# The experts' gather: plain float32 tokens, or their two rounded parts

## The chip, the cores and the metric

The kernel runs on one core of one Trainium2 chip. The metric is the device time of one execution in microseconds (us); the kernel before has a median of 2643.16 us over three runs. TensorE (PE in the profile) multiplies, VectorE (DVE) and ScalarE (ACT) work element by element, GpSimd (POOL) does little here, and SyncE (SP) issues the transfers from HBM.

## The reference

The program is two small models in a row, on 256 tokens of width 1024. The change lies in the last layer of the first, a mixture of eight experts. Cut to that:

```
def moe_ffn(h, router, w_gu, w_down):
    logits = (h @ router).astype(jnp.float32)
    top_val, top_idx = lax.top_k(logits, TOP_K)
    weights = jax.nn.softmax(top_val, axis=-1)
    gate = jnp.sum(jax.nn.one_hot(top_idx, N_EXPERTS, dtype=jnp.float32) * weights[..., None], axis=-2)
    out = jnp.zeros(h.shape, jnp.float32)
    for e in range(N_EXPERTS):
        out = out + gate[..., e:e + 1] * swiglu(h, w_gu[e], w_down[e])
    return out
```

`h` is the normed input, modulated: `rmsnorm(x, norm_w) * (1 + scale) + shift`. Two of eight experts (TOP_K) take each token; an expert is 1024 to 2 x 3584 and 3584 to 1024. All inputs and outputs are float32.

## The kernel before

The kernel is a row of stages; `experts` (L2362) is the fifth. Each engine runs its own function per stage (`tensor`, `vector`, `scalar`, `sync`), in program order, and semaphores tie them together: `e.wait_ge(*M.v.at(("Pe", x)))` waits until VectorE has passed the event of that name.

Products are made exact enough by splitting. A weight unit of 128x2048 float32 is copied by ScalarE to the rounded type fp32r (`split_hi`, L351; the high part) and VectorE subtracts that from the original (`split_lo`, L363; the low part). TensorE multiplies high x high, high x low and low x high in fp32r. Weights come from HBM through three slots of 2 MB; a slot comes free when VectorE has made the low part of its last unit, and a part's buffer comes free when TensorE has used it (three buffers of each).

Each expert works on at most 128 of the 256 tokens. Which ones is decided once: TensorE multiplies the tokens with the router (`routed_tensor`, L2665), VectorE ranks the logits into `sel` and takes the positions of the chosen tokens into `pos` (`routed_vector`, L2691). From `sel` and `pos` VectorE makes, for each expert, `Pe`, a [128, 2, 128] matrix of zeros and ones (L2384, `gather_vector`): row t has a one in column s where token t is the expert's s-th. TensorE then

- transposes Pe (`gather_tensor`, step 1), for putting the results back later, and
- gathers (steps 2 and 3, L2446): for each of 8 column tiles k and each half hf of the tokens, `xn[:, hf, k]` is the stationary operand and `Pe[:, hf, :]` the moving one, both plain float32; the two halves add up in PSUM. One step is a block of four k, 8 products.

VectorE scales and shifts the gathered columns into `XGf` (step 3 and 4) and the two parts `XGh`, `XGl` are made from it (step 5), which the expert's weight products use.

Order: for the first expert all of these steps come one after another, ahead of any weight product. For the others `coming` (L2627) puts step l-29 behind the down-projection's unit l of the expert before, so that a block of gather products stands in TensorE's queue between weight products. An expert has 42 units (28 of the up-projection, 14 of the down-projection), 12 weight products of 512 columns each. `round_tensor`, `round_scalar` and `round_vector` (L2632 to L2663) write this order out. A second round over the experts runs only if one expert has more than 128 tokens, and it isn't run on these inputs.

Ahead of the rounds, `scalar` (L2789) and `vector` (L2805) norm the tokens into `xn`, and modulate the transposed tokens into `HT` for the router (`turned_half`, L2758, one half of the pieces each); ScalarE and VectorE split weight unit 0 still earlier, and unit 1 right after `turned_half`.

Of the kernel before, what the change touches and what calls it, by code (L numbers as in the profile page):

```python
# [6 lines left out]
F32 = mybir.dt.float32  # L7
R32 = mybir.dt.float32r
AF = mybir.ActivationFunctionType
AX = mybir.AxisListType  # L10

D = 1024
# [502 lines left out]
def norm_scalar(c, e, S, ready):  # L515

    e.wait_ge(*c.first.g.at("eps"))
    e.table()
    for h in range(2):
        e.wait_ge(*ready[h])  # L520
        e.activation(c.xn[:, h, :], c.X[:, h, :], AF.Square, accum_out=c.ssq[:, h:h + 1]).then_inc(*S.a.up())
        e.wait_ge(*S.a.now())
        e.activation(c.rst[:, h:h + 1], c.ssq[:, h:h + 1], AF.Ln, scale=1.0 / D, bias=c.eps[:, :]).then_inc(*S.a.up())
        e.wait_ge(*S.a.now())
        e.activation(c.rst[:, h:h + 1], c.rst[:, h:h + 1], AF.Exp, scale=-0.5).then_inc(*S.a.up(("rst", h)))
# [1836 lines left out]
def experts(c):  # L2362
# [3 lines left out]
    io, K, X, xn, ones, gates = c.io, c.K, c.X, c.xn, c.ones, c.gates  # L2366
    before = c.mamba
    M = c.moe = Stage(c, "moe")
# [12 lines left out]
    hTh, hTl = c.put(40.5, "ehTh", [128, 28, 128], R32), c.put(54.5, "ehTl", [128, 28, 128], R32)  # L2381
    XGh, XGl = c.put(106.5, "XGh", [128, KC, 128], R32), c.put(110.5, "XGl", [128, KC, 128], R32)
    XGf, Y = HT[:, 0:4, :].rearrange("p a (b s) -> p (a b) s", s=128), HT[:, 4:8, :].rearrange("p a b -> p (a b)")
    Pe = c.put(68.5, "Pe", [128, 2, 128])  # L2384
    hrow = [c.put(70.5 + 2 * i, f"hrow{i}", [128, 512]) for i in range(2)]
    router_landed, norm_landed, raw_landed = c.event_signal("router_landed", 16), c.event_signal("final_norm_landed", 16), c.event_signal("raw_landed", 16)
    fn = gates[1]
# [43 lines left out]
    def gather_tensor(e, S, blk, x, step):  # L2431
        if step == 1:
            ps = ubanks.take((S.name, "PT", x))
            e.wait_ge(*ps.was)
            e.wait_ge(*S.v.at(("Pe", x)))
            for hf in range(2):
                m = e.transpose(ps.t[:, hf * 128:(hf + 1) * 128], Pe[:, hf, :], K["ident"])
            m.then_inc(*S.t.up(("PT", x)))
        if step in (2, 3):
            k0 = 4 * (step - 2)  # L2440
            ps = ubanks.take((S.name, "XG", x, k0))
            e.wait_ge(*ps.was)
            e.wait_ge(*S.v.at(("Pe", x)))
            for k in range(k0, k0 + 4):
                for hf in range(2):
                    m = e.matmul(ps.t[:, (k - k0) * 128:(k - k0 + 1) * 128], xn[:, hf, k * 128:(k + 1) * 128], Pe[:, hf, :], hf == 0, hf == 1)  # L2446
            m.then_inc(*S.t.up(("XG", x, k0)))

    def gather_vector(e, S, blk, x, step):
# [29 lines left out]
    def gather_scalar(e, S, blk, x, step):  # L2479
        if step == 5:  # L2480
            if x:
                e.wait_ge(*S.t.at(("row", x - 1, 6, 1)))
            for k0 in (0, 4):
                e.wait_ge(*S.v.at(("XGf", x, k0)))
                e.activation(XGh[:, k0:k0 + 4, :], XGf[:, k0:k0 + 4, :], AF.Copy).then_inc(*S.a.up(("XGh", x, k0)))
# [94 lines left out]
    def use_scalar(e, S, n):  # L2580
        x, l = at(n)
        if l < 28:
            j = l // 4
            if l % 4 == 1 and j:
                hidden_scalar(e, S, x, j - 1)
            if l % 4 == 3:
                ps = c.psum.of((S.name, "row", x, j, 0))
                e.wait_ge(*S.t.at(("row", x, j, 0)))
                if j > 1:
                    e.wait_ge(*S.t.at(("hT", x, j - 2)))  # L2590
                elif x:
                    e.wait_ge(*S.t.at(("hT", x - 1, 6 - j % 2)))
                e.activation(hrow[j % 2][:, :], ps.t[:, :], AF.Silu).then_inc(*S.a.up(("silu", x, j)))
                c.psum.leave((S.name, "row", x, j, 0), S.a)
        elif l == 28:
            hidden_scalar(e, S, x, 6)

    def use_vector(e, S, n):
        x, l = at(n)
        if l < 28:  # L2600
            j = l // 4
            if l % 4 == 1 and j:
                hidden_vector(e, S, x, j - 1)
            if l % 4 == 3:
                ps = c.psum.of((S.name, "row", x, j, 1))
                e.wait_ge(*S.t.at(("row", x, j, 1)))
                e.wait_ge(*S.a.at(("silu", x, j)))
                e.tensor_tensor(hrow[j % 2][:, :], hrow[j % 2][:, :], ps.t[:, :], ALU.mult).then_inc(*S.v.up(("h", x, j)))
                c.psum.leave((S.name, "row", x, j, 1), S.v)
            if l == 3 and x:  # L2610
                put_vector(e, S, x - 1)
            return
        if l == 28:
            hidden_vector(e, S, x, 6)
        if l == PER - 1 and (x < NE - 1 or S is again):
            summed_vector(e, S, x)
# [10 lines left out]
    def coming(n):  # L2627

        x, l = at(n)
        return (x + 1, l - 29) if 29 <= l < 35 and x + 1 < NE else None  # L2630
# [10 lines left out]
    def round_scalar(e, S, W, blk, begun):  # L2641
        for n in range(NU + AHEAD):
            if (EARLY if S is M else 0) <= n < NU:
                W.split_hi(e, n)
            if n == AHEAD - 1:
                begun(e)
            if n >= AHEAD:
                use_scalar(e, S, n - AHEAD)
                if coming(n - AHEAD):
                    gather_scalar(e, S, blk, *coming(n - AHEAD))  # L2650

    def round_vector(e, S, W, blk, begun):
        for n in range(NU + AHEAD):
            if (EARLY if S is M else 0) <= n < NU:
                W.split_lo(e, n)
            if n == AHEAD - 1:
                begun(e)
            if n >= AHEAD:
                use_vector(e, S, n - AHEAD)
                if coming(n - AHEAD):  # L2660
                    gather_vector(e, S, blk, *coming(n - AHEAD))
# [76 lines left out]
    def second(e, signals, otherwise=None):  # L2738

        e.wait_ge(*M.v.at("flag"))  # L2740
        return e.only_if(fli[0:1, 0:1], [s.at("end") for s in signals], otherwise)
# [16 lines left out]
    def turned_half(e, S, sig, dve):  # L2758

        e.wait_ge(*c.side.v.at(("mod", "moe", "cols")))  # L2760
        for n in ((0, 2) if dve else (1, 3)):
            h, k0 = n // 2, n % 2 * 4
            hs = slice(h * 128, (h + 1) * 128)
            ps = c.psum.of((S.name, "turned", n))
            e.wait_ge(*S.t.at(("turned", n)))
            for k in range(4):
                o, i = HT[:, k0 + k, hs], ps.t[:, k * 128:(k + 1) * 128]
                if dve:
                    e.tensor_scalar(o, i, s1[:, k0 + k:k0 + k + 1], ALU.mult, s2[:, k0 + k:k0 + k + 1], ALU.add).then_inc(*sig.up(("HT", n)))
                else:  # L2770
                    e.activation(o, i, AF.Identity, scale=s1[:, k0 + k:k0 + k + 1], bias=s2[:, k0 + k:k0 + k + 1]).then_inc(*sig.up(("HT", n)))
            c.psum.leave((S.name, "turned", n), sig)
# [16 lines left out]
    def scalar(e):  # L2789
        e.wait_ge(*before.t.at(("y", 7)))  # L2790
        for n in range(EARLY):
            U.split_hi(e, n)
        norm_scalar(c, e, M, [before.v.at(("X", h)) for h in range(2)])
        before.wait_for(e, "end")
        turned_half(e, M, M.a, False)
        round_scalar(e, M, U, 0, routed_scalar)
        M.a.mark("end")
        with second(e, [again.a]):
            M.wait_for(e, "end")
            round_scalar(e, again, U2, 1, lambda e: [gather_scalar(e, again, 1, 0, s) for s in range(6)])  # L2800
        again.a.mark("end")
        e.wait_ge(*again.v.at("end"))
        norm_scalar(c, e, again, [M.v.at(("X_half", h)) for h in range(2)])

    def vector(e):  # L2805
        norm_vector(c, e, M, 1)
        before.wait_for(e, "end")
        turned_half(e, M, M.v, True)
        round_vector(e, M, U, 0, routed_vector)
        begun = M.v.n  # L2810

        def last_put():
            M.v.n = begun
            summed_vector(e, M, NE - 1)
            put_vector(e, M, NE - 1)
            M.v.mark("end")

        with second(e, [again.v], last_put):
            last_put()
            M.wait_for(e, "end")  # L2820
            round_vector(e, again, U2, 1, lambda e: [gather_vector(e, again, 1, 0, s) for s in range(6)])
            put_vector(e, again, NE - 1)
        again.v.mark("end")
        e.wait_ge(*norm_landed.at("norm"))
        for h in range(2):
            e.wait_ge(*again.a.at(("rst", h)))
            e.scalar_tensor_tensor(X[:, h, :], X[:, h, :], c.rst[:, h:h + 1], fn[:, :], ALU.mult, ALU.mult).then_inc(*again.v.up(("X", h)))
# [990 lines left out]
```

## Time and profile before

| | |
|---|---|
| median of 3 runs | 2643.16 us (2642.90 to 2644.75) |
| the profiled execution | 2645.73 us, its span 2643.9 us |
| TensorE busy | 2432.2 us, 92% of the span |
| VectorE busy | 1984.5 us, 75% |
| ScalarE busy | 1431.7 us, 54% |
| read from HBM | 605 MB, 229 GB/s over the span |
| the experts' stage | about 776 to 1812 us |

The profile is of one execution. Busy time is the sum of an engine's instructions; a matmul's end is modelled and matmuls are pipelined, so that the start of one to the start of the next tells what it costs, not its duration. LDWEIGHTS (PEld) is the load of the stationary operand, 128x128 here, which TensorE can do while an earlier matmul streams. The granted clock is a share of 2.4 GHz.

### The profile page before, as it was taken

How to read it: one execution, taken by the hardware profiler on the slowest of the kernel's cores; microseconds unless marked ns; L12 is line 12 of the kernel's file. 1: busy time of each engine (PE TensorE's matmuls, PEld its weight loads, DVE VectorE, ACT ScalarE, POOL GpSimd, SP SyncE). 2: the span in 40 equal slices, each digit the busy share in tenths (PEclk: the TensorE clock that was granted, in tenths of full speed). 3: DMA queues.
4: the chain of work that ended last, by engine and by line, in shares of the span. 5: the costliest groups of instructions: out<-in, count | busy, mean ns of one | idle time of the engine just before them, and what ended most of it. 6: DMA issues, size and time to landing. Idle time of an engine off the chain costs nothing.

```text
span 2643.9 us, 32969 instructions
## 1 busy us (share of the span) xinstructions
PE 2432.2 (92%) x13898; PEld 2108.3 (80%) x13898; DVE 1984.5 (75%) x2208; ACT 1431.7 (54%) x1594; POOL 209.3 (8%) x261
## 2 busy tenths in 40 slices
PE   4877899898889999999999999998897999897998
PEld 3756799787777888888888888887887997886997
DVE  6756777686657898888888989886666775767675
ACT  3312443464546776767676767674444653344562
POOL 1101001000000000000000000001311110221110
PEclk8886899897889999999999999999998999998999
DMA  9652678432256999999999999995224453323552
GB/s 318 216 196 88 215 271 302 158 139 81 96 182 232 348 360 347 358 348 360 352 356 337 369 338 367 342 365 191 69 96 159 164 190 134 108 76 118 195 184 77
DMA packets 263558, 608.44 MB, mean 230 GB/s; under 512 B 18472, under 2 KB 33082, under 8 KB 263402
## 3 DMA queue, kind: packets, MB, share of 16 engines
q1 hardware_dynamic: 247808, 554.39, 58.4%
q0 software_dynamic: 14640, 51.49, 5.8%
q8 instruction: 111, 1.82, 0.3%
q10 hardware_dynamic: 954, 0.37, 0.1%
q14 instruction: 45, 0.37, 0.0%
HBM read 605.17 MB, written 1.05 MB: 229 GB/s over the span
## 4 chain that ended last, share of the span: by engine, by line
PE 80%; DVE 10%; ACT 5%; DMA 2%; issue 1%; POOL 1%; SPq 0%; PEldq 0%; PEld 0%; DVEq 0%; ACTq 0%; POOLq 0%
PE ps L132 78%; PE ps L136 2%; DVE eb L153 1%; DMA slots<-in_hyb_mod_w 1%; DVE X L153 1%; ACT L142 1%; DMA beside<-in_dense_mod_w 1%; DVE ul_in L145 1%; DVE macc L153 1%; DVE xn L153 1%; ACT uh_ffn L139 0%; ACT eb L139 0%; ACT xn L139 0%; DVE ul_ssm_w L145 0%; DVE gate L153 0%
## 5 line engine op out<-in xcount | busy, mean ns | idle before, releaser
L145 DVE TENSOR_TENSOR ul_moe_w<-slots,uh_moe_w 128x2048 fp32r<-128x2048 f32 x334 | 762.6, 2290 | 108.7 <-ACT uh_moe_w L139 108.4
L139 ACT ACTIVATE uh_moe_w<-slots 128x2048 fp32r<-128x2048 f32 x334 | 640.2, 1917 | 215.8 <-PE ps L132 187.4
L132 PE MATMUL ps<-uh_moe_w,XGh 128*128 128x512 f32 x896 | 356.7, 398 | 3.1 <-DVE XGl L145 2.1
L132 PE MATMUL ps<-uh_moe_w,XGl 128*128 128x512 f32 x896 | 349.5, 390 | 0.0
L132 PE MATMUL ps<-ul_moe_w,XGh 128*128 128x512 f32 x896 | 349.0, 389 | 0.0
L145 DVE TENSOR_TENSOR ul_ffn<-slots,uh_ffn 128x2048 fp32r<-128x2048 f32 x62 | 142.1, 2292 | 101.1 <-ACT uh_ffn L139 101.1
L132 PE MATMUL ps<-HTf,uh_ffn 128*128 128x256 f32 x704 | 201.5, 286 | 2.8 <-DVE HTlf L145 2.8
L132 PE MATMUL ps<-HTlf,uh_ffn 128*128 128x256 f32 x704 | 201.0, 285 | 0.0
L132 PE MATMUL ps<-HTf,ul_ffn 128*128 128x256 f32 x704 | 200.9, 285 | 0.0
L132 PEld LDWEIGHTS ps<-uh_moe_w,XGh 128*128 128x128 f32 x896 | 168.3, 188 | 39.1 <-DVE XGl L145 2.2
L132 PEld LDWEIGHTS ps<-uh_moe_w,XGl 128*128 128x128 f32 x896 | 168.2, 188 | 35.8
L132 PEld LDWEIGHTS ps<-ul_moe_w,XGh 128*128 128x128 f32 x896 | 168.5, 188 | 35.1 <-issue 1.7
L139 ACT ACTIVATE uh_ffn<-slots 128x2048 fp32r<-128x2048 f32 x66 | 125.7, 1911 | 96.4 <-PE ps L132 96.4
L132 PE MATMUL ps<-uh_moe_w,ehTh 128*128 128x512 f32 x448 | 177.2, 396 | 0.0
L132 PE MATMUL ps<-ul_moe_w,ehTh 128*128 128x512 f32 x448 | 174.7, 390 | 0.0
L132 PEld LDWEIGHTS ps<-HTf,uh_ffn 128*128 128x128 f32 x704 | 137.1, 195 | 3.6 <-DVE HTlf L145 3.6
L132 PE MATMUL ps<-uh_moe_w,ehTl 128*128 128x512 f32 x448 | 138.1, 389 | 0.0
L132 PEld LDWEIGHTS ps<-HTlf,uh_ffn 128*128 128x128 f32 x704 | 137.2, 195 | 0.0
L132 PEld LDWEIGHTS ps<-HTf,ul_ffn 128*128 128x128 f32 x704 | 137.0, 195 | 0.0
L132 PE MATMUL ps<-HTm,uh_in 128*128 128x256 f32 (+1 forms) x352 | 106.0, 301 | 6.1 <-DVE ul_in L145 3.0
L145 DVE TENSOR_TENSOR ul_dense_w<-slots,uh_dense_w 128x2048 fp32r<-128x2048 f32 x33 | 75.5, 2291 | 45.0 <-ACT uh_dense_w L139 45.0
L145 DVE TENSOR_TENSOR ul_ssm_w<-slots,uh_ssm_w 128x1024 fp32r<-128x1024 f32 (+1 forms) x57 | 68.6, 1204 | 54.0 <-ACT uh_ssm_w L139 53.9
(509 smaller groups left out, 5576.4 us busy)
## 6 DMA issues: line engine op xcount, KB each, us to landing
slots<-in_moe_w_gu SPq DMA_DIRECT2D x111, 2048.0 KB, 8.8
slots<-in_moe_w_down SPq DMA_DIRECT2D x56, 2048.0 KB, 7.9
slots<-in_w_up SPq DMA_DIRECT2D x20, 2048.0 KB, 7.9
slots<-in_w_in SPq DMA_DIRECT2D x14, 2048.0 KB, 8.5
slots<-in_dense_w_gu SPq DMA_DIRECT2D x10, 2048.0 KB, 9.9
slots<-in_ssm_w_in SPq DMA_DIRECT2D x10, 2048.0 KB, 8.0
slots<-in_w_down SPq DMA_DIRECT2D x10, 2048.0 KB, 7.8
slots<-in_dense_w_down SPq DMA_DIRECT2D x5, 2048.0 KB, 12.7
```

The costliest lines, as they stand in the source:

```text
L132: return self.e.matmul(o, lhsT, rhs, start=start, stop=stop, skip_group_check=skip) if self.e else DONE
L136: return self.e.transpose(o, i, ident[0:n, 0:n]) if self.e else DONE
L139: return self.e.activation(o, i, f, **kw) if self.e else DONE
L142: return self.e.preload_act_table_set("natural_log_exp_and_others") if self.e else DONE
L145: return self.e.tensor_tensor(o, a, b, op) if self.e else DONE
L153: return self.e.scalar_tensor_tensor(o, a, s, b, op0, op1) if self.e else DONE
```

## The change

The tokens `xn` are split once, as the weights are: ScalarE copies each half into `xh` (fp32r), and VectorE subtracts that from `xn` into `xl` (fp32r). Both get places of 8 KB per partition. In the gather each product with `xn` becomes two, one with `xh` and one with `xl`, and the four of a column tile add up in PSUM. `Pe` is declared fp32r, and its transpose reads it as float32. ScalarE's two copies stand between `turned_half` and its round, VectorE's two subtractions too, behind a wait for TensorE's last transposes of `xn` and for the copies. TensorE waits for the subtractions ahead of each block (after the first time, the wait is left out).

```
-    Pe = c.put(68.5, "Pe", [128, 2, 128])
+    Pe = c.put(68.5, "Pe", [128, 2, 128], R32)
+    xh, xl = c.put(118.25, "xnh", [128, 2, D], R32), c.put(126.25, "xnl", [128, 2, D], R32)
...
-                m = e.transpose(ps.t[:, hf * 128:(hf + 1) * 128], Pe[:, hf, :], K["ident"])
+                m = e.transpose(ps.t[:, hf * 128:(hf + 1) * 128], Pe[:, hf, :].bitcast(F32), K["ident"])
...
             e.wait_ge(*ps.was)
+            e.wait_ge(*M.v.at("xl"))
             e.wait_ge(*S.v.at(("Pe", x)))
             for k in range(k0, k0 + 4):
+                o, cs = ps.t[:, (k - k0) * 128:(k - k0 + 1) * 128], slice(k * 128, (k + 1) * 128)
                 for hf in range(2):
-                    m = e.matmul(ps.t[:, (k - k0) * 128:(k - k0 + 1) * 128], xn[:, hf, k * 128:(k + 1) * 128], Pe[:, hf, :], hf == 0, hf == 1)
+                    e.matmul(o, xh[:, hf, cs], Pe[:, hf, :], hf == 0, False)
+                    m = e.matmul(o, xl[:, hf, cs], Pe[:, hf, :], False, hf == 1)
...
         turned_half(e, M, M.a, False)
+        for h in range(2):
+            e.wait_ge(*M.v.at(("xn", h)))
+            e.activation(xh[:, h, :], xn[:, h, :], AF.Copy).then_inc(*M.a.up(("xh", h)))
         round_scalar(e, M, U, 0, routed_scalar)
...
         turned_half(e, M, M.v, True)
+        e.wait_ge(*M.t.at(("turned", 3)))
+        for h in range(2):
+            e.wait_ge(*M.a.at(("xh", h)))
+            e.tensor_tensor(xl[:, h, :], xn[:, h, :], xh[:, h, :].bitcast(F32), ALU.subtract).then_inc(*M.v.up("xl"))
         round_vector(e, M, U, 0, routed_vector)
```

## Rows read from the trace of the kernel before

**Rows 1.** The page: busy time and share by engine; the chain by line.
```profile
PE 2432.2 (92%) x13898; PEld 2108.3 (80%) x13898; DVE 1984.5 (75%) x2208; ACT 1431.7 (54%) x1594; POOL 209.3 (8%) x261
...
PE ps L132 78%; PE ps L136 2%; DVE eb L153 1%; DMA slots<-in_hyb_mod_w 1%; DVE X L153 1%; ACT L142 1%; DMA beside<-in_dense_mod_w 1%; DVE ul_in L145 1%; DVE macc L153 1%; DVE xn L153 1%; ACT uh_ffn L139 0%; ACT eb L139 0%; ACT xn L139 0%; DVE ul_ssm_w L145 0%; DVE gate L153 0%
```

**Rows 2.** Busy time by stretch of the experts' stage (one of six like stretches).
```profile
core 0: us, PE busy (x) PEld busy (x) DVE busy (x) ACT busy (x) POOL busy (x), PEclk, DMA share, GB/s
...
930.00:1054.00 124.00, 124.00 (x570) 101.42 (x569) 110.22 (x76) 86.78 (x58) 0.00 (x0) 1.00 0.96 352
```

**Rows 3.** Waits from 780 to 1800 us: us in total, times, longest.
```profile
ACT uh_moe_w L139 <- PE ps L132: 187.4, 240, 3.9
...
PE ps L132 <- DVE XGl L145: 2.1, 1, 2.1
```

**Rows 4.** Timeline of the stage's start: start, us, engine, line, instructions [idle before].
```profile
781.04 2.72 DVE L150 TENSOR_SCALAR HT<-ps,s_moe 128x128 f32<-128x128 f32 x8
...
784.64 1.92 ACT L139 ACTIVATE uh_moe_w<-slots 128x2048 fp32r<-128x2048 f32 x1
...
784.86 6.96 PE L132 MATMUL ps<-rw,HT 128*128 128x8 f32 x32 [1.64 <-issue]
786.59 2.29 DVE L145 TENSOR_TENSOR ul_moe_w<-slots,uh_moe_w 128x2048 fp32r<-128x2048 f32 x1 [2.82 <-ACT uh_moe_w L139]
788.91 0.37 SPq L177 DMA_DIRECT2D slots<-in_moe_w_gu  x1
791.86 0.17 DVE L156 COPY L<-ps 128x16 f32<-128x16 f32 x1 [2.98 <-PE ps L132]
...
796.43 0.60 DVE L150 TENSOR_SCALAR Pe<-k_iota,epos,esel 128x128 f32<-128x128 f32 x2
...
797.57 5.63 PE L132 MATMUL ps<-Pe,xn 128*128 128x128 f32 x32
...
805.26 0.50 PE L132 MATMUL ps<-uh_moe_w,XGh 128*128 128x512 f32 x1 [2.06 <-DVE XGl L145]
...
805.83 0.40 PE L132 MATMUL ps<-uh_moe_w,XGl 128*128 128x512 f32 x1
...
806.06 0.40 PE L132 MATMUL ps<-uh_moe_w,XGh 128*128 128x512 f32 x1
```

**Rows 5.** The gather's products: ns min/median/max; one steady block in time.
```profile
L132 PEld LDWEIGHTS ps<-Pe,xn x256: 187/192/337, 797.4 to 1654.2; 128*128 128x128 f32 x128
L132 PE MATMUL ps<-Pe,xn x256: 270/275/421, 797.6 to 1654.3; 128*128 128x128 f32 x128
...
897.50 1.95 PE L132 MATMUL ps<-Pe,xn 128*128 128x128 f32 x16
899.20 0.48 PE L132 MATMUL ps<-uh_moe_w,ehTh 128*128 128x512 f32 x1
```

**Rows 6.** The page's group of weight loads with XGl: busy us, mean ns.
```profile
L132 PEld LDWEIGHTS ps<-uh_moe_w,XGl 128*128 128x128 f32 x896 | 168.2, 188 | 35.8
```

**Rows 7.** The second model's attention in time: plain products that stream 64 columns.
```profile
1967.50 1.90 PE L132 MATMUL ps<-vbt,PTm 128*128 128x64 f32 x16
1969.20 0.47 PE L132 MATMUL ps<-uh_in,HTm 128*128 128x512 f32 x1
```

**Rows 8.** Router products, then first gather, by stretch (columns end as rows 2).
```profile
784.86:791.80 6.94, 6.94 (x32) 6.86 (x32) 0.00 (x0) 0.50 0.25 62
...
797.36:803.20 5.84, 5.84 (x34) 5.65 (x33) 0.00 (x0) 0.64 0.00 0
```

**Rows 9.** A stretch of 48 rounded products of 256 columns: TensorE, clock, DMA.
```profile
1819.34:1825.10 5.76, 5.76 (x50) 1.00 0.12 44
```

**Rows 10.** A copy to fp32r and a subtraction of 128x1024: ns min/median/max.
```profile
L139 ACT ACTIVATE uh_in<-slots x58: 256/1046/1062, 1809.0 to 2387.0; 128x1024 fp32r<-128x1024 f32 x56, 128x64 fp32r<-128x64 f32 x2
L145 DVE TENSOR_TENSOR ul_in<-slots,uh_in x58: 225/1218/1592, 1809.3 to 2388.1; 128x1024 fp32r<-128x1024 f32 x56, 128x64 fp32r<-128x64 f32 x2
```

**Rows 11.** A stretch around the first gather, columns as rows 2.
```profile
797.00:805.30 8.30, 6.15 (x35) 5.96 (x35) 3.79 (x11) 1.29 (x3) 0.00 (x0) 0.73 0.00 0
```

## The prediction

> **What bounds the kernel now.** I read the page first. TensorE is busy 92% of the span, and the chain that ended last lies for 78% of it on the one line that issues every matmul [rows 1]. The change touches the experts' stage, so the busy time by stretches is next: in each of six like stretches from 930 to 1674 us TensorE is busy for all of the 124 us, at a granted clock of 1.00 (2.4 GHz), while the DMA engines are busy 96 to 97% of the time, VectorE about 110 us and ScalarE about 87 us [rows 2]. The waits of the stage say the same from the other side: ScalarE waits 187.4 us for TensorE to release a weight buffer, while the longest wait of TensorE's weight products is one of 2.1 us, at the very start [rows 3]. So in steady state what ends last is TensorE, with the transfers close behind; time on TensorE counts in full there, time on VectorE or ScalarE counts only when it eats up the lead that they have. The start of the stage is different. There the chain hops: VectorE modulates, TensorE computes the router's logits (6.94 us), VectorE ranks, TensorE counts positions, VectorE builds Pe, TensorE gathers, and TensorE's first weight product starts only at 805.26 [rows 4]. On that stretch every engine's latency is on the path, unless it lies beside the logits.
>
> **The change part by part.**
>
> *1. The product itself, on TensorE.* The loop runs 8 experts x 2 blocks of four column tiles; a block has 4 x 2 products of a 128x128 tile of tokens with a 128x128 tile of Pe. That is 128 plain products, and the trace has 256 weight loads and 256 matmuls for them [rows 5]: a plain float32 product is two load-and-stream records. The change replaces each by two products of the rounded type, and those have one record each (the experts' weight products with XGl: 8 experts x 28 units x 4, and 896 records [rows 6]). So a block has 16 records before and 16 records after. The question is what one record costs with 128 columns.
> Before, a block in steady state takes from 897.50 to 899.20, 1.70 us, or 106 ns a record [rows 5]. Two things could set that: streaming (two passes over 128 columns) or loading 128x128 weights. The trace separates them: in the second model's attention, plain products stream only 64 columns against 128x128 weights, half the streaming, and 16 records again take from 1967.50 to 1969.20, 1.70 us [rows 7]. The router's products stream 8 columns and take 6.94/32 = 217 ns a record at the granted clock 0.50 (1.2 GHz), which is 108 ns at 2.4 GHz [rows 4, 8]. So 106 ns is the floor that a 128-column weight load sets, whatever is streamed behind it. A load for rounded operands lasts 188 ns on average, one for plain float32 has a median of 192 ns [rows 5, 6]; nothing there says that a rounded load is shorter.
> No row shows a rounded product over 128 columns; all have 256 or 512. That price is bounded from both sides. Upper end: 48 rounded products of 256 columns take from 1819.34 to 1825.10, 120 ns each [rows 9], and fewer columns should not cost more. Lower end: 512 columns cost 227 ns (805.83 to 806.06 [rows 4]), 256 cost 120 ns, so 107 ns per 256 columns; taking off another 128 gives 67 ns, if the load did not count. I take 106 ns, from the 64-column rows, because there too the stream is shorter than the load, as it would be here. Then each block stays at 1.70 us and the part is worth 0. With the upper end a block costs 16 x 0.014 = 0.22 us more; seven experts in steady state have 14 blocks, 3.1 us, and the first expert's two blocks (32 records in 5.63 us [rows 4], at a clock of 0.64 over the stretch [rows 8]) grow by 0.13 of that, 0.7 us: +3.8 us. With the lower end a record saves 0.039 us: 14 x 16 x 0.039 = 8.7 us, and 0.37 x 5.63 = 2.1 us at the start: -10.8 us.
> One rule speaks against this value. The Trainium skill, "TensorE: Matmul & The Clock Gate", section "Back-to-back issue gap", puts load-and-matmul pairs at about 81 ns for 128 columns and 131 ns for 512; by that the sum would be an estimate of 14 x 16 x 0.025 + 1.3 = 6.9 us less. For 512 columns this trace has 227 ns, not 131, so I do not carry its 81 over.
>
> *2. The two parts, made once.* ScalarE gets two copies of 128x1024 to the rounded type and VectorE two subtractions of that size; the same two forms for the second model's input weights take 1046 and 1218 ns (medians) [rows 10]. ScalarE's copies stand right ahead of its split of weight unit 1, which starts at 784.64 now [rows 4]. Both copies: 784.7 to 786.8; unit 1's high part then ends near 788.8 instead of 786.56. VectorE ends its transposed tokens at 783.76, subtracts from 785.8 to 788.25, and makes unit 1's low part from 788.8 to 791.1 instead of 786.59 to 788.88. Next on VectorE is the copy of the logits, at 791.86, which waits for TensorE [rows 4]. The whole part hides beside the 6.94 us of logits with 0.8 us to spare; ScalarE's next work is an exponential that needs those logits. If that cover were gone, the added time on VectorE would be up to 2 x 1.22 us, on the path. VectorE's new wait for the last transposes has ended before its own last modulated tile, and TensorE's new wait for the two subtractions (done at 788.25, its gather begins at 797.57) ends long before. What is queued behind VectorE's wait for the copies is only unit 1's low part, already counted.
> Its consequence on the transfer queue: the refill of slot 0, issued at 788.91 when unit 1's low part was done [rows 4], goes out some 2.2 us later. Nothing is queued up behind it: the DMA engines are idle from 797 to 805.3, all through the gather (share 0.00 [rows 11]). Landing 2.2 us later, it only fills a part of that. Zero; two microseconds if it mattered.
>
> *3. Pe as a rounded tile.* Zeros and ones are the same numbers. Writing it is the same tensor_scalar on VectorE, 0.60 us for two [rows 4]. If writing the rounded type were twice as slow, it would be 0.6 us on the first expert's path, and nothing later, where a Pe is built while TensorE has weight products queued; at the other end it is 0. As many elements are written as before and the transposes read the same bits, so I take 0.1 us, near the lower end.
>
> **The sum.** 0 (product) + 0 (parts) + 0 (refill) + 0.1 (Pe) = +0.1 us on the profiled execution's 2645.73 us (span 2643.9 and 1.8 around it). The median of the runs shown is 2643.16; the forecast against it is 2643.3.
>
> **The rivals.**
> *A, slower: a rounded product over 128 columns costs what the plain one costs.* TensorE may take its single-pass rate for the rounded type only for long streams; every rounded product in this kernel streams 256 or 512 columns [rows 6, 9], so the trace can't exclude it. Its place is the gather, its price is the plain product's, two records or 213 ns, instead of one: a block doubles from 1.70 to 3.40 us, 14 x 1.70 = 23.8 us, and the first pair adds 5.6 us: +29.4 us, 2672.6. It decides as soon as a rounded 128-column product takes over 130 ns (14 x 16 x 0.024 us = 5.3 us). For it: no row excludes it. Against it: a rounded 256-column product takes 120 ns, little more than one pass of 256 columns, so no pass is hidden in the type itself.
> *B, faster: the rounded load overlaps.* If rounded weights load behind the preceding stream more fully, a record falls towards 67 ns and the total by up to 10.8 us, to 2632.4. The transfers would not stop it: at 96 to 97% busy they leave some 3% of a stretch of 124 us, 3.7 us, and B wants 1.3 us of that. (By the 81 ns of the Trainium skill, "TensorE: Matmul & The Clock Gate", section "Back-to-back issue gap", the time would be an estimate of 2636; no run here shows it.) For B: in weight products a load of 188 ns lies wholly behind a 227 ns stream. Against: with short streams no row of 128 weight columns falls below 106 ns.
> *C, the split at the start is not covered.* The margin is 0.8 us; a late copy on ScalarE would push the logits' copy by up to 2 us. This stays within the forecast's own range.
>
> **How the numbers follow.** The forecast (no change, C included) gets 0.70, A 0.18, B 0.12. The forecast's own range is 2640 (records a little cheaper) to 2649 (+3.8 for 120 ns records and +2 for C). Adding B takes the low end to 2632, and then 0.18 is left out, so the range is 2632 to 2649; A's 2673 lies outside it. A measurement of this kernel can tell about 0.2%, 5.3 us: the forecast's case is inside that but for its edges. So: faster 0.13 (B), same 0.68, slower 0.19 (A, and the edge at 120 ns with C).
>
> **What would show it.** In the trace after, Pe's group should have 256 records again, half with xnh and half with xnl, plus the 16 of the transposes. A steady block should take 1.7 us between the weight products around it; 1.07 would be B, 3.4 A. The logits' copy on VectorE should still wait for TensorE, with unit 1's low part ending near 791, and the first weight product should start 20.4 us after the first router product, within 0.3 us (784.86 and 805.26 [rows 4]). The last expert's last gather load, now at 1654.2 [rows 5], should again come 848.9 us after the first weight product. The prediction is wrong if the record isn't bound by its load, or if the stage is bound by its transfers after all, in which case even A or B would be partly hidden.

## The result and the profile after

The changed kernel has a median of 2651.99 us over 22 runs, the kernel before 2642.78 us over 22 on the same chip: a ratio of 1.0031, interval 1.0017 to 1.0045. In this measurement it is slower, the interval lying above 1.000, and the time is outside the range of 2632 to 2649. The same kernel was measured twice more (below): 1.0007 (0.9993 to 1.0021) and 1.0017 (0.9997 to 1.0037). Neither of these two can be told from no change by itself, and either ratio times 2643 us would lie inside the range. The three intervals overlap from 1.0017 to 1.0021, 4.5 to 5.5 us. What all three profiles of the changed kernel show is 3.7 to 3.8 us, in the stage's start, and the low clock that goes with it ends within 30 us of the router's first product.

The gather's products first, as in [rows 5]: their group, then one steady block and the weight product behind it, all in the changed kernel.

```profile
L132 PEld LDWEIGHTS ps<-Pe,xnh x128: 187/192/337, 799.5 to 1660.2; 128*128 128x128 f32 x128
L132 PE MATMUL ps<-Pe,xnh x128: 220/274/455, 799.6 to 1660.3; 128*128 128x128 f32 x128
...
L132 PEld LDWEIGHTS ps<-Pe,xnl x128: 187/192/333, 799.7 to 1660.3; 128*128 128x128 f32 x128
L132 PE MATMUL ps<-Pe,xnl x128: 274/276/415, 799.8 to 1660.4; 128*128 128x128 f32 x128
...
903.37 0.22 PE L132 MATMUL ps<-Pe,xnh 128*128 128x128 f32 x1
903.43 0.28 PE L132 MATMUL ps<-Pe,xnl 128*128 128x128 f32 x1
903.54 0.27 PE L132 MATMUL ps<-Pe,xnh 128*128 128x128 f32 x1
...
904.99 0.28 PE L132 MATMUL ps<-Pe,xnl 128*128 128x128 f32 x1
905.10 0.45 PE L132 MATMUL ps<-uh_moe_w,ehTh 128*128 128x512 f32 x1
905.39 0.40 PE L132 MATMUL ps<-ul_moe_w,ehTh 128*128 128x512 f32 x1
```

There are 256 records again. A block takes from 903.37 to 905.10, 1.73 us; before it was 1.70 us. A rounded product of 128 columns costs 111 ns (903.43 to 904.99 are 14 of them); a plain record in the gathers of the kernel before starts 108 to 112 ns after the one before it, with a median of 112. The steady state is as it was: VectorE makes Pe for the second and the eighth expert 750.85 us apart; in the kernel before the same two start at 893.80 and 1644.43, 750.63 us apart.

```profile
899.67 0.60 DVE L150 TENSOR_SCALAR Pe<-k_iota,epos,esel 128x128 fp32r<-128x128 f32 x2
...
1650.52 0.60 DVE L150 TENSOR_SCALAR Pe<-k_iota,epos,esel 128x128 fp32r<-128x128 f32 x2
```

Now the start of the stage, the timeline that answers [rows 4].

```profile
786.80 2.01 ACT L139 ACTIVATE xnh<-xn 128x1024 fp32r<-128x1024 f32 x2
...
787.02 6.96 PE L132 MATMUL ps<-rw,HT 128*128 128x8 f32 x32 [1.64 <-issue]
787.97 2.36 DVE L145 TENSOR_TENSOR xnl<-xn,xnh 128x1024 fp32r<-128x1024 f32 x2 [2.04 <-ACT xnh L139]
...
790.64 2.29 DVE L145 TENSOR_TENSOR ul_moe_w<-slots,uh_moe_w 128x2048 fp32r<-128x2048 f32 x1 [0.31 <-ACT uh_moe_w L139]
792.96 0.37 SPq L177 DMA_DIRECT2D slots<-in_moe_w_gu  x1
794.02 0.17 DVE L156 COPY L<-ps 128x16 f32<-128x16 f32 x1 [1.09 <-PE ps L132]
...
798.60 0.60 DVE L150 TENSOR_SCALAR Pe<-k_iota,epos,esel 128x128 fp32r<-128x128 f32 x2
...
799.60 0.46 PE L132 MATMUL ps<-Pe,xnh 128*128 128x128 f32 x1
799.85 0.41 PE L132 MATMUL ps<-Pe,xnl 128*128 128x128 f32 x1
...
808.72 0.80 PE L132 MATMUL ps<-uh_moe_w,XGh 128*128 128x512 f32 x1 [2.06 <-DVE XGl L145]
809.32 0.63 PE L132 MATMUL ps<-ul_moe_w,XGh 128*128 128x512 f32 x1
809.74 0.63 PE L132 MATMUL ps<-uh_moe_w,XGl 128*128 128x512 f32 x1
...
814.00 0.39 PE L132 MATMUL ps<-uh_moe_w,XGh 128*128 128x512 f32 x1
814.23 0.39 PE L132 MATMUL ps<-ul_moe_w,XGh 128*128 128x512 f32 x1
```

The parts hide as forecast: the copy of the logits still waits for TensorE, 1.09 us. From the router's first product to the first gather product it is 12.58 us, before 12.71. From there to the first weight product it is 9.12 us (799.60 to 808.72), before 7.69 (797.57 to 805.26 [rows 4]). And the first weight products are 427 ns apart instead of 227; they reach 230 ns only at 814.00. The windows say what that is. Each of the next two fences has a stretch from the first gather product to the first weight product, and the four microseconds behind it; the granted clock stands third from the end. The changed kernel:

```profile
799.60:808.72 9.12, 7.06 (x34) 6.88 (x33) 3.75 (x10) 1.25 (x3) 0.00 (x0) 0.50 0.05 18
808.72:812.72 4.00, 4.00 (x9) 3.15 (x10) 3.78 (x9) 1.81 (x2) 0.00 (x0) 0.50 0.00 0
```

The kernel before:

```profile
797.57:805.26 7.69, 5.63 (x34) 5.44 (x33) 3.75 (x10) 1.25 (x3) 0.00 (x0) 0.74 0.00 0
805.26:809.26 4.00, 4.00 (x17) 3.30 (x18) 3.79 (x9) 2.74 (x3) 0.00 (x0) 1.00 0.00 0
```

Before, the clock rises from 1.2 to 2.4 GHz inside the first gather, 4.0 us behind its first product (0.74 on average), and the weight products start at 2.4. After, it stays at 0.50 through the gather and through the first five microseconds of weight products (to 813.97). So the profiled execution's 9.0 us more (2652.9 against 2643.9) divide, by the starts of the same instructions in both, into

| from | to | before | after | difference |
|---|---|---|---|---|
| start of the span | router's first product | 784.86 | 787.02 | +2.16 |
| router's first product | first weight product | 20.40 | 21.70 | +1.30 |
| first weight product | Pe of the second expert | 88.54 | 90.95 | +2.41 |
| Pe of the second expert | Pe of the eighth | 750.63 | 750.85 | +0.22 |
| Pe of the eighth | transposes of X for the next model | 164.56 | 165.20 | +0.64 |
| those transposes | end of the span | 834.91 | 837.18 | +2.27 |

The second and third rows are the stage's start, 3.71 us. The first and last stretches run unchanged code. Whether they, too, belong to the change is what the repeats had to tell. They tell it for the last: it takes 834.7 and 834.6 us in the two repeats, no longer than in the kernel before.

### The profile page after: what moved, and what is told of

It is laid out like the page before. It is cut to its first block, busy times and chain, and to the rows that moved or that the text cites. A ratio compares the mean times of both kernels' runs of the same rounds, so it can differ in the third digit from the quotient of the medians.

```text
span 2652.9 us, 32974 instructions
## 1 busy us (share of the span) xinstructions
PE 2440.6 (92%) x13898; PEld 2113.0 (80%) x13898; DVE 1987.0 (75%) x2210; ACT 1433.4 (54%) x1596; POOL 209.3 (8%) x261
## 4 chain that ended last, share of the span: by engine, by line
PE 80%; DVE 10%; ACT 5%; DMA 2%; issue 1%; POOL 1%; SPq 0%; DVEq 0%; ACTq 0%; POOLq 0%
PE ps L132 78%; PE ps L136 2%; DVE eb L153 1%; DVE X L153 1%; DMA slots<-in_hyb_mod_w 1%; ACT L142 1%; DVE macc L153 1%; DVE xn L153 1%; DVE ul_in L145 1%; DMA beside<-in_dense_mod_w 1%; ACT xn L139 1%; ACT eb L139 0%; DVE ul_moe_w L145 0%; DVE ul_ssm_w L145 0%; DVE gate L153 0%
```

## The experiments

The theory after the comparison: both gathers keep the same pace, but a rounded product streams 128 columns behind its load where a plain record streams two passes of 128, and TensorE's clock does not rise on that here. The two passes can be read where the stream is long enough to set the pace: the products that put an expert's result back are plain and stream 512 columns, and their records are 0.43 us apart at a granted clock of 1.00 ((3.59 - 0.59)/7), where a rounded product of 512 columns takes 0.227 us. In the kernel before, the group and one such stretch:

```profile
L132 PE MATMUL ps<-HT,PTe x64: 590/592/697, 939.2 to 1803.9; 128*128 128x512 f32 x64
...
939.20 3.59 PE L132 MATMUL ps<-HT,PTe 128*128 128x512 f32 x8
```
The rivals: the added copies and subtractions (with the refill that they delay); a small loss in each steady block; the chance of the moment at which the clock rises; and, for the clock itself, the operand type instead of what is streamed.

**The changed kernel again (e1_rep_after, e9_rep_after2), and the kernel before again (e10_rep_before).** No edit.

> The changed kernel once more. The profile of it had TensorE's granted clock at 0.50 (1.2 GHz) through the whole first gather, and until 812 to 816 us, while the kernel before rose to 2.4 GHz halfway through its first gather. Theory 1 (clock at the start): rounded products of 128 columns stream half as much as plain ones behind each load, and the clock stays at 1.2 GHz longer; the clock over the first gather is again 0.50, the first gather takes 6.9 us or more from its first to its last product, and the ratio to before is 1.001 to 1.005. Rival (chance of the moment): the clock rises somewhere else in each execution, here in the middle of the gather as before.

> The changed kernel a third time, to narrow the ratio (1.0031 and 1.0007 so far, one interval each). What the profiles show inside the stage is 3.7 us of 2643, 1.0014: if that is all, this ratio lies around it, 1.000 to 1.003; if the change also costs something outside what the profiles of the stage show, it lies at 1.003 again. Clock in the profile: 0.50 until 26 us after the router's first product, once more.

> The kernel before, measured against itself: how far a ratio strays with no change at all. 1.000 by construction; an estimate outside 0.999 to 1.001 would say that the ratios of this study carry a spread of the size of the whole effect. The stage's profile: clock up from 16 us after the router's first product, 7.7 us from gather to weights, 88.5 us to the second expert's Pe.

Measured: e1 1.0007 (0.9993 to 1.0021), a little under what I had expected, e9 1.0017 (0.9997 to 1.0037), and for the kernel before against itself 0.9993 (0.9973 to 1.0013). In means the changed kernel is 3.8 and 4.3 us above the kernel before measured beside it (2646.2 against 2642.5, 2648.5 against 2644.1); in the first measurement it was 9.3 us. Both new profiles of the changed kernel repeat the start of the stage to within a few hundredths: 9.13 and 9.13 us at a clock of 0.50, then 90.91 and 90.97 us to the second expert's Pe. The profile of the kernel before repeats its own, 7.64 and 88.55 us. The windows of e9_rep_after2 and of e10_rep_before:

```profile
799.94:809.07 9.13, 7.07 (x35) 6.88 (x33) 3.76 (x10) 1.25 (x3) 0.00 (x0) 0.50 0.06 22
809.07:813.07 4.00, 4.00 (x9) 3.13 (x10) 3.79 (x9) 1.81 (x2) 0.00 (x0) 0.50 0.00 0
```

```profile
788.35:795.99 7.64, 5.58 (x33) 5.39 (x32) 3.76 (x10) 1.25 (x3) 0.00 (x0) 0.75 0.00 0
795.99:799.99 4.00, 4.00 (x18) 3.31 (x19) 3.78 (x9) 2.77 (x3) 0.00 (x0) 1.00 0.00 0
```

So it is no chance of the single profile; the 3.7 to 3.8 us come in all three profiles of the changed kernel. The moment is the same in all of them: in each of the ten profiles without extra products the clock fell to 0.50 between 19.8 and 20.0 us ahead of the first gather product, so these profiles compare like with like, but at one timing only; e7 and e8 below have another.

**The parts without their use (e2_parts_only).** The copies and subtractions stay; all products take `xn`.

```diff
+                    if True:
+                        m = e.matmul(o, xn[:, hf, cs], Pe[:, hf, :].bitcast(F32), hf == 0, hf == 1)
+                        continue
                     e.matmul(o, xh[:, hf, cs], Pe[:, hf, :], hf == 0, False)
                     m = e.matmul(o, xl[:, hf, cs], Pe[:, hf, :], False, hf == 1)
```

> The two parts are made as in the changed kernel, but every gather product takes the plain float32 tokens as before. Theory 1 (the clock, from the products): within 0.1% of before, since the splits hide beside the router's products. Theory 2 (the added work and the refill that goes out 4 us later): slower by 0.15 to 0.3%, as the changed kernel, with the clock in the first gather as in the kernel before.

Measured: 0.9988 (0.9973 to 1.0004); 7.70 us at a mean clock of 0.74, then 88.55 us. The added work, the delayed refill and Pe as a rounded tile add nothing: from the router's first product to the second expert's Pe it is 108.97 us, before 108.94. That rival is out.

```profile
794.94:802.64 7.70, 5.64 (x34) 5.45 (x33) 3.75 (x10) 1.25 (x3) 0.00 (x0) 0.74 0.05 19
802.64:806.64 4.00, 4.00 (x17) 3.29 (x18) 3.78 (x9) 2.75 (x3) 0.00 (x0) 1.00 0.00 0
```

**The first expert plain, the others rounded (e3_first_plain), and the mirror of it (e4_first_rounded).** The edit of e2 with `if x == 0:` in the one and `if x > 0:` in the other, in the place of `if True:`.

> The changed kernel, but the first expert's 16 products are plain float32 ones again; the 112 of the other seven are rounded. Theory 1 (clock at the start): within 0.1% of before, the clock rises inside the first gather. Theory 3 (the rounded products cost a little in steady state, 14 blocks): slower by some 0.2%, as the changed kernel. From the second expert's Pe to the eighth's 750.6 to 750.9 us by theory 1, and 752 or more by theory 3.

> The mirror of it: only the first expert's products are rounded, the other seven experts' plain. Theory 1: as slow as the changed kernel (ratio 1.0015 or more), clock 0.50 through the first gather, 91 us from the first weight product to the second expert's Pe instead of 88.5. Theory 3: within 0.1% of before.

Measured: e3 1.0003 (0.9989 to 1.0017), e4 1.0005 (0.9992 to 1.0018). The ratios alone don't separate the two: e4's is lower than the 1.0015 expected, and both intervals hold no change as well as the whole 3.7 us. The profiles do separate them. With 112 of the 128 products rounded, e3 has the start of the kernel before (7.67 us, then 88.54), and from the second expert's Pe to the eighth's it takes 750.67 us, against 750.63 with plain products. With 16 rounded, e4 has the whole loss: 9.13 and 90.97 us, and 750.36. From the router's first product to the transposes of X, where the first row of the table ends and the last begins, it is 1024.1 us in the kernel before and 1023.8 in its repeat, 1024.1 in e3, 1023.8 in e2, and 1027.7 in e4, 1028.7 in the first profile of the changed kernel, 1027.8 and 1027.9 in its two repeats. The loss inside the stage is the first expert's alone. The two profiles, e3 first:

```profile
787.24:794.91 7.67, 5.61 (x34) 5.42 (x33) 3.75 (x10) 1.25 (x3) 0.00 (x0) 0.74 0.06 21
```

```profile
794.27:803.40 9.13, 7.07 (x35) 6.88 (x33) 3.75 (x10) 1.25 (x3) 0.00 (x0) 0.50 0.06 24
```

**What the clock follows (e5_first_wide, e6_first_narrow).** The first expert's products only, with the other streaming width. In the changed kernel they stream both halves of Pe:

```diff
+                    if x == 0:
+                        e.matmul(ps.t[:, 0:256], xh[:, hf, cs], Pe[:, :, :].rearrange("p h t -> p (h t)"), hf == 0, False)
+                        m = e.matmul(ps.t[:, 0:256], xl[:, hf, cs], Pe[:, :, :].rearrange("p h t -> p (h t)"), False, hf == 1)
+                        continue
```

In the kernel before they stream half of one:

```diff
-                    m = e.matmul(ps.t[:, (k - k0) * 128:(k - k0 + 1) * 128], xn[:, hf, k * 128:(k + 1) * 128], Pe[:, hf, :], hf == 0, hf == 1)
+                    w = 64 if x == 0 else 128
+                    m = e.matmul(ps.t[:, (k - k0) * 128:(k - k0) * 128 + w], xn[:, hf, k * 128:(k + 1) * 128], Pe[:, hf, 0:w], hf == 0, hf == 1)
```

> The changed kernel, but the first expert's 32 rounded products stream both halves of Pe, 256 columns instead of 128, behind the same 32 weight loads (into one place, so what the first expert gathers isn't the reference's). If the clock follows how much TensorE streams, not the type: the granted clock rises within the first gather, as in the kernel before, with 0.8 to 0.9 in the two microseconds from 16 us after the router's first product on, and from the first gather product to the first weight product it takes about 7.7 us instead of 9.1. Rival (the clock follows the plain float32 type, or its two-record form): the clock stays at 0.50 for 26 us after the router's first product, as in the changed kernel.

> The kernel before, plain float32 throughout, but the first expert's products stream 64 columns of Pe instead of 128 (half of its gathered columns are left out). By the loads, a product costs the same; it streams half as much. If the clock follows what is streamed: it stays at 0.50 through the gather, which takes about 9.1 us to the first weight product, and the second expert's Pe comes 91 us after that. Rival (the type): as the kernel before, 7.7 us and 88.5 us.

Of each there is one execution, its profile, and the whole times are not compared. e5, rounded and wide:

```profile
798.76:806.71 7.95, 5.90 (x34) 5.69 (x32) 3.75 (x10) 1.25 (x3) 0.00 (x0) 0.74 0.06 23
806.71:810.71 4.00, 4.00 (x18) 3.31 (x19) 3.78 (x9) 2.77 (x3) 0.00 (x0) 1.00 0.00 0
```

e6, plain and narrow:

```profile
795.89:804.88 8.99, 6.93 (x33) 6.74 (x32) 3.76 (x10) 1.25 (x3) 0.00 (x0) 0.50 0.00 0
804.88:808.88 4.00, 4.00 (x9) 3.14 (x10) 3.78 (x9) 1.81 (x2) 0.00 (x0) 0.50 0.00 0
```

They change places. The rounded gather that streams twice as much behind the same 32 loads brings the clock up like the plain one, and the plain gather that streams half as much leaves it at 0.50 like the rounded one. In both slow cases, e6 and the changed kernel, TensorE counts as busy without a gap (6.93 and 7.06 us) and starts a record every 213 ns, as the plain gather does until its clock rises. So the type alone is out, and so are the busy time and the number of loads; what differs between the two sides is how much is streamed behind each load.

**Streams put into the gaps (e7_warm_before, e8_warm_after, e11_fill_before, e12_fill_after).** Products whose results nobody reads, in PSUM banks that later real products overwrite (the form of e11 and e12; in e7 and e8 it has no `w`):

```diff
+    def warm(e, ps, n, w=128):
+        hi, _ = U.parts(e, 0)
+        for _ in range(n):
+            e.matmul(ps.t[0:w, :], hi[:, 0, 0:w], hi[:, 0, :])
```

In e7 and e8: 4 ahead of the router's products, 4 behind them, 2 ahead of Pe's transposes. In e11 and e12: 4 ahead, then one with w=4 (4 weight columns) after every second router product, 8 with w=4 behind them, and 4 with w=4 ahead of the transposes.

> The kernel before, with ten extra products of 512 rounded columns, whose results nobody reads, put where TensorE sits idle at the start of the stage: 4 ahead of the router's products, 4 while VectorE ranks, 2 while it builds Pe. If the clock follows what is streamed, it rises before the first gather starts; the gather then takes 3.6 us instead of 5.6, and from the router's first product to the second expert's Pe it is 2 us shorter than 108.9. Rival: the idle gaps between keep it at 1.2 GHz, and the stage is as long or, where the extra products outlast a gap, up to 1.5 us longer.

> The same ten extra products in the changed kernel. If the low clock at the start is its whole loss, they give it back: from the router's first product to the second expert's Pe as in the kernel before with the same products, within 0.5 us, and the ratio to before is 0.998 to 1.0005. Rival (the rounded gather keeps the clock low whatever ran ahead of it): the clock is 0.50 in the gather again and the first weight products run at 1.2 GHz for some 4 us.

> The kernel before with products nobody reads, now also between the router's products: 4 of 128 x 512 ahead, then one of 4 weight columns x 512 after every second router product, 8 more while VectorE ranks, 4 while it builds Pe. If the clock falls back in the router's products because they stream almost nothing, it now stays at 2.4 GHz: the router's products with the 8 extra ones take 5.3 us instead of 7, everything to the first weight product 15 to 17 us instead of 20.4, and the ratio is 0.997 to 0.999. Rival: the gaps in which TensorE waits for VectorE bring the clock down anyway, and the extra products are pure cost, 18 us or more.

> The same extra products in the changed kernel. If the first gather starts at 2.4 GHz, its 32 rounded products take 3.5 us as in steady state, and the change costs nothing: from the router's first product to the second expert's Pe as in the kernel before with the same extra products, within 0.5 us. Rival: the rounded gather streams too little to hold the clock, which then falls in or right after it, and the first weight products run at 1.2 GHz: 1.5 to 3 us longer than that kernel.

| | ratio (interval) | router to gather | gather to weights | to the second Pe | sum |
|---|---|---|---|---|---|
| before | | 12.71 | 7.69 | 88.54 | 108.94 |
| after | 1.0031 (1.0017 to 1.0045) | 12.58 | 9.12 | 90.95 | 112.65 |
| e7, before with 10 | 0.9985 (0.9968 to 1.0001) | 10.00 | 7.34 | 88.53 | 105.87 |
| e8, after with 10 | 1.0008 (0.9991 to 1.0026) | 11.40 | 9.13 | 89.89 | 110.42 |
| e11, before, filled | 0.9988 (0.9970 to 1.0006) | 9.38 | 5.79 | 90.13 | 105.30 |
| e12, after, filled | 1.0005 (0.9989 to 1.0022) | 10.39 | 9.13 | 90.37 | 109.89 |

The expectations of e7, e8 and e12 missed. In e7 the clock was up for 3.4 us in the router's products, fell again 7.0 us ahead of the gather and rose only 3.2 us into it, not ahead of it. In e8 it fell 8.4 us ahead of the gather and then stayed at 0.50 until 3.0 us into the weight products, so the two gathers differ at this timing too. And I had expected the changed kernel to catch up in e8 and e12; it stays 4.6 us behind its partner in both pairs. The windows of e11 (first) and e12: the plain gather of e11 starts at 2.4 GHz and keeps it (32 records in 3.6 us), and the clock falls 1.5 us into the weight products, behind the wait for XGl, for 3.4 us; in e12 it fell 0.55 us before the gather began, and the rounded gather doesn't bring it back.

```profile
792.45:798.24 5.79, 3.73 (x34) 3.54 (x32) 3.75 (x10) 1.25 (x3) 0.00 (x0) 1.00 0.32 119
798.24:802.24 4.00, 4.00 (x13) 3.20 (x13) 3.78 (x9) 1.82 (x2) 0.00 (x0) 0.69 0.00 0
```

```profile
797.82:806.95 9.13, 7.07 (x35) 6.88 (x33) 3.76 (x10) 1.25 (x3) 0.00 (x0) 0.50 0.30 115
806.95:810.95 4.00, 4.00 (x10) 3.14 (x11) 3.79 (x9) 1.81 (x2) 0.00 (x0) 0.50 0.00 0
```

Part of the 4.6 us is not the clock's. The router's products are shorter with the extra ones around them (4.6 us in e11 and e12 instead of 7), and now VectorE's added work is no longer covered: its copy of the logits, with which the ranking starts, comes 4.88 us behind the router's first product in e11 and 5.84 us in e12, where it follows the low part of unit 1 without any wait for TensorE. e11 first:

```profile
783.07 0.36 PE L132 MATMUL ps<-rw,HT 128*128 128x8 f32 x2
787.95 0.17 DVE L156 COPY L<-ps 128x16 f32<-128x16 f32 x1 [0.86 <-PE ps L132]
```

```profile
787.43 0.36 PE L132 MATMUL ps<-rw,HT 128*128 128x8 f32 x2
793.27 0.17 DVE L156 COPY L<-ps 128x16 f32<-128x16 f32 x1
```

That is 1.0 us of the 4.6, and in e8 against e7, in the same way, 1.4 us (11.40 against 10.00 in the table). What the prediction called C is real, then, as soon as the cover is gone. Since TensorE waits longer ahead of the gather in e12 than in e11, the pair doesn't tell whether a rounded gather would hold a clock that is up; that stays open. From the router to the second Pe e7 and e11 take 3.1 and 3.6 us less than the kernel before; their intervals just reach 1.000, so a gain in the whole time is likely but not shown.

## Why the prediction was wrong

**The product's price was right.** Forecast 106 ns a record between 67 and 120; measured 111. Forecast 1.70 us a block, measured 1.73. The 106 was 1.70 us divided by 16, the short first step behind a long stream counted in; from record to record a plain one takes 112 ns too. Rival A (a doubled price, 2673 us) and rival B (down to 67 ns, 2632 us) both needed another pace and are out. That the load sets this pace is the reading that fits: 128 rounded columns and 64 or 128 plain ones all give 111 or 112 ns.

**The parts and Pe were right.** The forecast left 0.8 us of cover beside the logits and the profile 1.09; the refill went out 1.9 us later, relative to the router's first product, and e2_parts_only shows no cost. The cover held because the router's products ran at 1.2 GHz; e8 and e12 show 1.0 to 1.4 us of cost where they are shorter. Pe is written in the same 0.60 us. Rival C is out for this kernel.

**The step that failed is "each block stays at 1.70 us and the part is worth 0", applied to the first expert's two blocks.** I had read in the rows that the first gather ran at a mean clock of 0.64 over its stretch [rows 8] while the router's products were at 0.50, and carried that clock over as if it were given. But a mean between the two levels means that the clock rose in that very stretch, and by e3 to e6 it is the gather's own streaming on which it rose: a record of before streams two passes of 128 columns behind one load, a changed one a single pass. The same pace for TensorE's records was not the same work for its clock. Measured in the place of 0: 1.4 us in the gather (32 records at 213 ns from the second on, instead of a mean of 176) and 2.4 us in the weight products behind it, the first dozen of which run at 427 ns instead of 227. The sum of the prediction had no term for the second at all: it took the gather's length as the only thing that the gather can change. Two of its own signs showed the miss: the first weight product came 21.70 us behind the first router product, not 20.4 within 0.3, and the last gather load 851.6 us behind the first weight product (1660.3 against 808.72), not 848.9.

**The range was built without it.** It came from the price of a record and the cover of C. The row that speaks of the clock, [rows 8], stood in the text only as a factor. Had the clock staying at 0.50 been priced, 32 x 0.217 us = 6.9 us in the place of 5.63 would have come from the rows at hand, 1.3 us. The 2.4 us behind it, 12 weight products 0.2 us longer each, would have needed a guess at how long the clock stays low. The 3.7 us together make 2647 us, which is inside the range and under the measured median. So this mechanism alone doesn't carry the time out of the range; the rest does, and no profile pins it on the change.

**What remains.** The first measurement's 1.0031 is 8.2 us, and 3.7 of them are shown. Weighted by their intervals, the three measurements give an estimate of 1.0019, within about 0.0009: 5 us, give or take 2.4, which holds the 3.7. The stretches outside the stage run the same code in both kernels and differ by several microseconds between profiles of one kernel. The largest of them is the state-space layer ahead of the experts. From its first product to its first output product, in the kernel before and in its repeat, e10_rep_before:

```profile
516.60:729.60 213.00, 185.40 (x1255) 167.85 (x1255) 146.47 (x291) 116.21 (x173) 11.03 (x15) 0.86 0.28 99
```

```profile
518.30:720.30 202.00, 174.34 (x1253) 159.33 (x1254) 146.07 (x291) 116.17 (x173) 11.04 (x15) 0.91 0.30 105
```

It takes 202 us in three of the fourteen profiles and 213 in eleven, with a mean clock of 0.91 and 0.86. An unequal share of these two lengths among the runs could move a median by a few microseconds: in the first measurement 9 of the 22 runs of the kernel before took under 2642 us and none between 2638.7 and 2642.6, while of the changed kernel 5 of 22 took under 2645.7 us, the same limit with the stage's 3.7 us added. That these runs had the short form is not shown, as only one run of each was profiled. The second and third measurements, at 1.0007 and 1.0017, lie around the 1.0014 that the stage gives. All six profiles in which every gather product was rounded happened to have the long form, so a tie between the change and the code ahead of it is not excluded; nothing in the profiles shows one.

## What to carry to other kernels

When a product is rewritten at an equal pace, look at where TensorE's clock rises in the profile, and ask which instructions stood just ahead of that point. If the edited ones are among them, price the edit once more with the clock left at 1.2 GHz, and count the work behind it too, for as long as the clock stays low there. And name what a hidden piece of work hides behind: if that gets shorter, as in e8 and e12, the piece is back on the path.

With 128-column operands a plain float32 product (two records of 112 ns) and two rounded ones (111 ns each) cost the same. Splitting such an operand into rounded parts gains nothing. By the same trace it would gain with a wider moving side: at 512 columns a plain product is two records of 0.43 us, two rounded ones take 0.227 us each.

## What the runs showed of the hardware

- A rounded product of 128 columns costs 111 ns at 2.4 GHz and 213 ns at 1.2 GHz, one record of a plain float32 product of 128 columns 108 to 112 and 213; two of the one cost as much as one of the other. At 512 columns and 2.4 GHz it is 227 ns for the rounded product and 0.43 us for one of the plain product's two records.
- TensorE busy without a gap for 6.9 to 7.1 us did not bring the clock up from 0.50, six times with rounded 128-column products (the changed kernel and its two repeats, e4, e8, e12) and once with plain 64-column ones (e6); with plain 128-column ones (before, e2, e3, e10) or rounded 256-column ones (e5) it rose 3.9 to 4.1 us into the gather. In all of these but e8 and e12 it had fallen some 20 us ahead of the gather.
- The state-space layer of this kernel takes 202 or 213 us with the same code, at a mean clock of 0.91 or 0.86, VectorE's and ScalarE's busy times being equal within 0.4 us in the two stretches shown.
